# Stick-breaking scores of two heads on the two row halves of TensorE's array, without zero padding

## The reference, cut to what matters

```python
z = jnp.einsum('bqhd,bshd->bhqs', q_blk, k, preferred_element_type=jnp.float32) * scale
valid = key_pos[None, :] < q_pos[:, None]
log_beta = jax.nn.log_sigmoid(z)
log_keep = jnp.where(valid, jax.nn.log_sigmoid(-z), 0.0)
log_keep_after = lax.cumsum(log_keep, axis=3, reverse=True) - log_keep
att = jnp.where(valid, jnp.exp(log_beta + log_keep_after), 0.0)
```

## Time and profile before

| | us |
|---|---|
| median of 3 runs | 1177.25 (1177.04 to 1177.65) |
| the profiled execution, its own time | 1177.26 |
| its span, first to last instruction | 1175.5 |
| TensorE busy | 1156.3 (98%) |
| DVE busy | 812.0 (69%) |
| ACT busy | 627.4 (53%) |
| GpSimd busy | 292.2 (25%) |

### The profile page before, as it was taken

The page is one execution under the profiler, slowest core; times in us unless marked ns, Lnnn a source line. Parts: engine busy times, 40 slices in busy tenths (PEclk is TensorE's granted clock), DMA queues, the critical chain, the costliest instruction groups (busy, mean ns, idle before and its releaser), DMA issues.

```text
span 1175.5 us, 18209 instructions
## 1 busy us (share of the span) xinstructions
PE 1156.3 (98%) x7410; PEld 1033.7 (88%) x7410; DVE 812.0 (69%) x874; ACT 627.4 (53%) x739; POOL 292.2 (25%) x282
## 2 busy tenths in 40 slices
PE   8999999999999999999999999999999999999996
PEld 6998988888998888888899888888889999888885
DVE  7686777675589667776558767766557767767653
ACT  5675565554455556555335656555446755655531
POOL 5000532211123354221111344221110005332221
PEclk9999999999999999999999999999999999999998
DMA  8743445555562345556553345555544335565541
GB/s 314 216 133 108 180 175 188 180 209 187 180 173 105 111 176 214 180 180 215 179 180 141 108 156 206 195 180 201 197 165 175 108 108 180 179 216 179 205 154 36
DMA packets 30828, 201.84 MB, mean 172 GB/s; under 512 B 3504, under 2 KB 4592, under 8 KB 7328
## 3 DMA queue, kind: packets, MB, share of 16 engines
q1 hardware_dynamic: 28800, 197.41, 47.4%
q0 software_dynamic: 352, 1.31, 0.9%
q10 hardware_dynamic: 1600, 2.02, 0.7%
HBM read 197.91 MB, written 1.84 MB: 170 GB/s over the span
## 4 chain that ended last, share of the span: by engine, by line
PE 94%; DVE 4%; ACT 1%; issue 0%; DMA 0%; POOL 0%; DVEq 0%; ACTq 0%
PE banks L1262 41%; PE banks L1266 21%; PE banks L1256 7%; PE banks L1258 7%; PE banks L1257 7%; PE banks L1250 4%; PE banks L1391 1%; PE banks L1333 1%; PE banks L1405 1%; DVE w_lo L831 1%; DVE x_split L837 1%; PE banks L1393 0%; PE banks L1541 0%; DVE small L1102 0%; DVE scratch L1099 0%
## 5 line engine op out<-in xcount | busy, mean ns | idle before, releaser
L812 DVE TENSOR_TENSOR w_lo<-raw,w_hi 128x2048 fp32r<-128x2048 f32 x180 | 440.9, 2452 | 201.6 <-ACT w_hi L476 201.5
L476 ACT ACTIVATE w_hi<-raw 128x2048 fp32r<-128x2048 f32 x183 | 349.4, 1909 | 95.3 <-PE banks L1266 47.2
L1262 PE MATMUL banks<-x_split,w_hi 128*128 128x512 f32 x1408 | 336.7, 391 | 0.0
L1262 PEld LDWEIGHTS banks<-x_split,w_hi 128*128 128x128 f32 x1408 | 258.5, 188 | 49.9
L1266 PEld LDWEIGHTS banks<-x_split,w_lo 128*128 128x128 f32 x1408 | 181.0, 191 | 7.1
L1266 PE MATMUL banks<-x_split,w_lo 128*128 128x256 f32 x1408 | 184.0, 283 | 0.0
L1262 PE MATMUL banks<-hid_split,w_hi 128*128 128x512 f32 x704 | 173.1, 391 | 0.0
L1262 PEld LDWEIGHTS banks<-hid_split,w_hi 128*128 128x128 f32 x704 | 127.4, 188 | 23.3
L1256 PE MATMUL banks<-x_split,w_hi 128*128 128x256 f32 x384 | 110.5, 288 | 0.0
L1257 PE MATMUL banks<-x_split,w_hi 128*128 128x256 f32 x384 | 108.6, 283 | 0.0
L1258 PE MATMUL banks<-x_split,w_lo 128*128 128x256 f32 x384 | 108.6, 283 | 0.0
(11 more groups left out here) (179 smaller groups left out, 1485.6 us busy)
## 6 DMA issues: line engine op xcount, KB each, us to landing
raw<-w SPq DMA_DIRECT2D x183, 1024.0 KB, 4.9
raw<-w SPq DMA_DIRECT2D x8, 256.0 KB, 6.9
x<-x_in SPq DMA_DIRECT2D x2, 512.0 KB, 5.7
raw<-w SPq DMA_DIRECT2D x2, 512.0 KB, 8.9
out<-x SPq DMA_DIRECT2D x4, 256.0 KB, 2.8
k_all<-k_all ACTq DMA_DIRECT2D x1, 960.0 KB, 12.3
rel_scratch<-rel_lut POOLq DMA_DIRECT2D x1, 768.0 KB, 10.6
rel_bias<-rel_scratch POOLq DMA_DIRECT2D x2, 256.0 KB, 9.0
```

The costliest lines, as they stand in the source:

```text
L476: act.activation(w_hi[slot][:, :], raw[slot][:, :], ACT.Copy).then_inc(hi_done, 1)
L812: dve.tensor_tensor(w_lo[slot][:, :], raw[slot][:, :], w_hi[slot][:, :].bitcast(FP32), ALU.subtract).then_inc(lo_done, 1)
L1262: return pe.matmul(pair(b), wt[0], xs, start=first, stop=False, skip_group_check=True)
```

## The change

The zeros go, and with them GpSimd's `query_zeros`. Queries and keys of a pair lie in one buffer `qk_both`, are split by one instruction on ACT and one on DVE into `qk_split`, and each head's score matmuls use only its own 64 rows (`own(h)`): 64 x 128 weights (the keys) on one row half of the array. The products are issued in twos: early keys of one head (256 columns) into the early bank and late keys of the other head into the late bank, on the other row half. The late ones have 128 queries; these are streamed twice, to 256 columns, and the second copy goes to a part of the bank that nobody reads. Three such twos cover early keys of head 0 and late keys of head 1. Then TensorE waits for its own two last matmuls (`z_half`), and three more cover early keys of head 1 and late keys of head 0. ACT's `soft` waits for the two last matmuls of the second group (`z`).

```diff
--- before.py
+++ after.py
@@ -127,8 +127,8 @@
         q_all = placed("q_all", [P, HEADS, SEQ], FP32, 0)
         k_all = placed("k_all", [P, HEADS, SEQ], FP32, 4 * HEADS * SEQ)
         v_all = placed("v_all", [P, 2, D], FP32, 8 * HEADS * SEQ)
-        q_split = placed("q_split", [P, 2, 2, SEQ], FP32R, 4 * KT * SEQ)
-        k_split = placed("k_split", [P, 2, SEQ], FP32R, 4 * HEADS * SEQ + 4 * KT * SEQ)
+        qk_both = placed("qk_both", [P, 2, SEQ], FP32, 0)
+        qk_split = placed("qk_split", [P, 2, 2, SEQ], FP32R, 4 * KT * SEQ)
         hid_split = placed("hid_split", [P, FFN_T, 2, SEQ], FP32R, 0)
         o_split = sb("o_split", [P, KT, 2, SEQ], FP32R)
         o_hi, o_lo = o_split[:, :, 0, :], o_split[:, :, 1, :]
@@ -275,12 +275,12 @@
         norm = signals("norm", "six x_new hi lo ss sums ms guess rstd")
         latent = signals("lat", "c_new hi lo ss sums ms guess rstd")
         mixer = [
-            signals("m0", "v_new qk_new q_zero k_hi q_hi k_lo q_lo z ln softplus sp_lo sums att av o_hi o_lo"),
+            signals("m0", "v_new qk_new qk_hi qk_lo z_half z ln softplus sp_lo sums att av o_hi o_lo"),
             signals("m1", "q_part q_new rope_tab rot_in krope_sum krope_new kfill k_part k_new v_part v_new logits max_new "
                           "exp_new sum_new inv_new p_new pt pt_new av o_hi o_lo"),
             signals("m2", "q_tmp q_new v_new v_part logits s_new s_max m_new exp_new sink_new r_new p_new pt pt_new av "
                           "o_hi o_lo"),
-            signals("m3", "v_new qk_new q_zero k_hi q_hi k_lo q_lo z ln softplus sp_lo sums att av o_hi o_lo"),
+            signals("m3", "v_new qk_new qk_hi qk_lo z_half z ln softplus sp_lo sums att av o_hi o_lo"),
         ]
         ffn = signals("ffn", "g_part g_free g_new u_part u_new silu scaled hid hi lo acc")
 
@@ -405,19 +405,6 @@
                             pool.tensor_scalar(pr[:, a, keys], pr[:, a, keys], s[:, 12 + 2 * late + a:13 + 2 * late + a],
                                                1.0, ALU.mult, ALU.mult).then_inc(m.p_new, 1)
 
-            def query_zeros(i):
-
-                if i:
-                    pool.wait_ge(norm.x_new, 16 * i)
-                pool.wait_ge(norm.ss, 2 * i + 1)
-                if i == 0:
-                    pool.wait_ge(cast_done, 2)
-                for h in range(2):
-                    if h:
-                        pool.wait_ge(mixer[i].q_zero, 1)
-                    pool.memset(q_split[others(h), :, h, :].bitcast(FP32), 0.0).then_inc(mixer[i].q_zero, 1)
-                pool.wait_ge(mixer[i].q_zero, 2)
-
             def swa_products():
                 m = mixer[2]
                 for g in range(GROUPS):
@@ -443,8 +430,6 @@
                 model_squares(2 * i)
                 if i == 0:
                     masks()
-                if i % 3 == 0:
-                    query_zeros(i)
                 if i == 0:
                     relative_bias()
                 if i == 1:
@@ -527,9 +512,7 @@
 
                 def qk_hi(p):
                     act.wait_ge(m.qk_new, 2 * p + 2)
-                    act.activation(k_split[:, 0, :], k_all[:, p, :], ACT.Copy).then_inc(m.k_hi, 1)
-                    for h in range(2):
-                        act.activation(q_split[own(h), 0, h, :], q_all[own(h), p, :], ACT.Copy).then_inc(m.q_hi, 1)
+                    act.activation(qk_split[:, 0, :, :], qk_both[:, :, :], ACT.Copy).then_inc(m.qk_hi, 1)
 
                 qk_hi(0)
                 split(b + 7)
@@ -540,7 +523,7 @@
                 def soft(p):
 
                     e, z = buf(0, 768), two_banks[p % 2][:, 0:768]
-                    act.wait_ge(m.z, p + 1)
+                    act.wait_ge(m.z, 2 * p + 2)
                     t = step(act.activation(e, z, ACT.Abs))
                     act.wait_ge(act_step, t)
                     t = step(act.activation(e, e, ACT.Exp, scale=-1.0))
@@ -907,21 +890,17 @@
 
                     dve.wait_ge(unit_used, b + 5 + p)
                     src = bank[4 + p % 2]
-                    dve.scalar_tensor_tensor(q_all[:, p, :], src[:, 0:SEQ], SB_SCALE, R, ALU.mult,
+                    dve.scalar_tensor_tensor(qk_both[:, 0, :], src[:, 0:SEQ], SB_SCALE, R, ALU.mult,
                                              ALU.mult).then_inc(m.qk_new, 1)
-                    dve.tensor_tensor(k_all[:, p, :], src[:, SEQ:512], R, ALU.mult).then_inc(m.qk_new, 1)
+                    dve.tensor_tensor(qk_both[:, 1, :], src[:, SEQ:512], R, ALU.mult).then_inc(m.qk_new, 1)
 
 
                 sp_hi, sp_lo = soft_split[:, 0, :], soft_split[:, 1, :]
 
                 def qk_low(p):
-                    dve.wait_ge(m.k_hi, p + 1)
-                    dve.tensor_tensor(k_split[:, 1, :], k_all[:, p, :], k_split[:, 0, :].bitcast(FP32),
-                                      ALU.subtract).then_inc(m.k_lo, 1)
-                    for h in range(2):
-                        dve.wait_ge(m.q_hi, 2 * p + h + 1)
-                        dve.tensor_tensor(q_split[own(h), 1, h, :], q_all[own(h), p, :],
-                                          q_split[own(h), 0, h, :].bitcast(FP32), ALU.subtract).then_inc(m.q_lo, 1)
+                    dve.wait_ge(m.qk_hi, p + 1)
+                    dve.tensor_tensor(qk_split[:, 1, :, :], qk_both[:, :, :], qk_split[:, 0, :, :].bitcast(FP32),
+                                      ALU.subtract).then_inc(m.qk_lo, 1)
 
                 qk(0)
                 qk_low(0)
@@ -1372,26 +1351,36 @@
 
                 def logits(p):
 
-                    early, late = score_banks(p)
+                    early, late = bank[2 * (p % 2)], bank[2 * (p % 2) + 1]
                     mask = head_blocks(mask_b[:, 0:512])[:, :, 0, :]
                     pe.matmul(head_blocks(early)[:, :, 0, :], ident_b[:, :], mask, start=True, stop=False,
                               skip_group_check=True)
-                    pe.matmul(late, ident_b[:, :], mask, start=True, stop=False, skip_group_check=True)
-                    if p == 0:
-                        pe.wait_ge(m.q_zero, 2)
-                    for key_low, query_low in ((0, 0), (1, 0), (0, 1)):
-                        if query_low:
-                            pe.wait_ge(m.q_lo, 2 * p + 2)
-                        elif key_low:
-                            pe.wait_ge(m.k_lo, p + 1)
-                        else:
-                            pe.wait_ge(m.q_hi, 2 * p + 2)
-                            pe.wait_ge(m.k_hi, p + 1)
-                        kk, qq = k_split[:, key_low, :], q_split[:, query_low, :, :]
-                        pe.matmul(early, kk[:, 0:P], qq.rearrange("p h s -> p (h s)"), start=False, stop=query_low == 1,
-                                  skip_group_check=True)
-                        last = pe.matmul(late, kk[:, P:SEQ], qq[:, :, P:SEQ], start=False, stop=query_low == 1,
+                    pe.matmul(late[:, 0:SEQ], ident_b[:, :], mask, start=True, stop=False, skip_group_check=True)
+
+                    def early_keys(h, key_low, query_low):
+                        return pe.matmul(early[:, SEQ * h:SEQ * h + SEQ], qk_split[own(h), key_low, 1, 0:P],
+                                         qk_split[own(h), query_low, 0, :], start=False, stop=query_low == 1,
                                          skip_group_check=True)
+
+                    def late_keys(h, key_low, query_low):
+                        twice = qk_split[own(h), query_low, 0, P:SEQ].unsqueeze(1).to_broadcast([HD, 2, P])
+                        spots = late[:, :].rearrange("p (d h q) -> p d h q", d=2, h=2)[:, :, h, :]
+                        return pe.matmul(spots, qk_split[own(h), key_low, 1, P:SEQ], twice, start=False,
+                                         stop=query_low == 1, skip_group_check=True)
+
+                    pe.wait_ge(m.qk_hi, p + 1)
+                    for first in range(2):
+                        if first:
+                            pe.wait_ge(m.z_half, 2 * p + 2)
+                        for key_low, query_low in ((0, 0), (1, 0), (0, 1)):
+                            if key_low and not first:
+                                pe.wait_ge(m.qk_lo, p + 1)
+                            one = early_keys(first, key_low, query_low)
+                            last = late_keys(1 - first, key_low, query_low)
+                        if not first:
+                            one.then_inc(m.z_half, 1)
+                            last.then_inc(m.z_half, 1)
+                    one.then_inc(m.z, 1)
                     last.then_inc(m.z, 1)
 
                 def keep_sums(p):
```

## The result

| | before | after |
|---|---|---|
| median, us | 1177.39 (1177.04 to 1177.73, 8 runs) | 1180.88 (1180.64 to 1181.23, 8 runs) |
| ratio to before | | 1.0030 (95% interval 1.0021 to 1.0039) |
| span of the profiled execution | 1175.5 | 1178.8 |

The change makes the kernel 3.5 us slower; forecast were 3.3. The spans of the two profiled executions differ by 3.3. The page after, busy engines, answers to the earlier trace rows: TensorE has 96 matmuls more (16 steps with 12 score matmuls instead of 6), DVE and ACT 32 instructions less each, GpSimd its four memsets less.

A forecast was written before the change was run, and what follows sets the result against it. TensorE, busy for 98% of the span, was taken as the bound. A step's scores take 1.24 us against 1.06; sixteen steps give +2.9, two returns at p = 0 +0.4, together +3.3: 1180.6 us, range 1175.2 to 1182.4.

The forecast's parts named there:

- the covers: Splits on ACT and DVE, GpSimd's zeros: hidden behind TensorE's `qk` work, so some 0.5 us less a pair is worth nothing.
- The overlap: Score matmuls on two row halves: two fp32r matmuls of 256 columns take the time of one, 0.12 us a pair.
- Rival 1: Score pairs: halves don't overlap in fp32r, a pair takes 0.24 us, 11.5 us more in all, 1192.1 us; chance 0.10.
- low end: Lower case of the sum: pace 0.11 at four places, release 0.03; +0.12 us a step, 1179.6 us in all.
- The change of division: From 128-row masks into half-row scores: load and drain not hidden, 0.20 us each, first pair 0.31 us behind the mask.
- The wait half-way: TensorE waits for its own matmuls between third and fourth pair: 0.45 us instead of 0.12.
- rival 2: Half-way wait nearly free: third to fourth pair 0.12 us, 1175.2 us in all; chance 0.10.
- rival 3: Fourth pair's weight loads pass the half-way wait: 0.11 us a step saved, 1178.8 us in all; chance 0.08.
- Rival 4: Neither the half-way wait nor the entry into the scores costs anything: 1171.6 us; chance 0.06, with anything else faster.
- the entry: New change of array division from the masks into the scores, 16 times, at 0.20 us.
- the release: Half-way wait, from the matmuls' modelled end to the held load: taken as 0.05 us, bounds 0.03 and 0.12.
- The sentence on the Trainium skill's rule (87 ns): Half-way wait: increments of concurrent tiles serialize, 87 ns for two of each instead of 0.05 us; total then 1181.2 us.

The follow-up runs named there:

- run 3: Changed kernel with three splits again on ACT and three on DVE instead of one each: 1180.67 us, ratio 1.0029.
- run 5: Changed kernel with the late queries streamed once (128 columns) instead of twice: 1180.85 us, ratio 1.0029.
- run 2: Changed kernel with both matmuls of a pair on one row half, late scores of the wrong head: 1191.51 us, ratio 1.0120.
- run 1: Changed kernel without half-way wait and bank hand-over; second group reuses the first's rows, half the scores of the wrong head: 1175.08 us, ratio 0.9982.
- run 10: Kernel before plus a TensorE wait for its own first product, the only wait ahead of the second (low-keys wait moved earlier): 1182.46 us, ratio 1.0044.
- run 4: Changed kernel with one increment instead of two at the half-way wait, on the last matmul alone: 1180.28 us, ratio 1.0026.
- run 6: Changed kernel with a bank for each head and no half-way wait, sums in four matmuls a part instead of three: 1177.54 us, ratio 1.0002.
- run 7: Version with a bank per head and no half-way wait, late queries also streamed once: 1176.48 us, ratio 0.9993 against the kernel before.
- run 8: Kernel before plus a TensorE wait, after its first product, for its own last matmul on 128 rows, one increment: 1183.58 us, ratio 1.0052.
- run 11: Changed kernel with one half-way increment, plus a long-met wait on another semaphore written behind the half-way wait: 1180.31 us, ratio 1.0026.

## Why the prediction was right

**The bound and the covers.** TensorE's order set the time, as the earlier trace rows said. The work taken off ACT and DVE is worth nothing (run 3). For GpSimd's zeros no run was made; before, nothing waited for them. Softplus's last piece is ready 1.04 us before the sums want it for p > 0, before 1.07. The second copy of the late queries slows nothing (run 5).

**The overlap** of two fp32r matmuls of 256 columns, which the trace of before showed only for plain fp32, holds: 0.12 us a pair, 0.24 on one half (run 2). Rival 1 is out, and its 11.5 us were 10.6. (The prediction's 0.78 us for 15 loads are 0.10 us per two and not 0.11; only its low end uses this.)

**The change of division** came out at the forecast 0.31 us from the mask to the first pair.

**The wait half-way** was right in kind. It is TensorE's wait for itself that costs, and the cost goes when wait and hand-over go (run 1: 5.8 us). The hand-over of banks is only why the kernel has the wait: without any hand-over and on 128 rows the wait costs 5.3 us, against 5.2 for the halves with the same single increment (run 10; run 4 less run 1). Rivals 2 and 3 are out: third to fourth pair are 0.47 us, not 0.12 or 0.34. Rival 4 goes with them, as both the wait and the entry cost what was forecast or more. What the prediction quotes of the Trainium skill for rival 3 asks for row groups that don't conflict, but the fourth pair uses the same two as the third, so it gave the rival less than the prediction says. The wait's size was forecast a little low. The term is the release, taken as 0.05 between bounds of 0.03 and 0.12; it measured 0.09, of which 0.03 belong to the second increment (run 4). The sentence on the Trainium skill's rule (87 ns) had the better number, and by it the sum was 1181.2.

**The sum.** The release was 0.04 us too small, but other parts of the step were a little too large (third to fourth pair 0.47, forecast 0.45), so the step from second mask to last pair grew by 0.20 us, not 0.18: 16 x 0.02 = 0.3 us more than forecast. On the other side a small stall vanished that the prediction had not seen. In the kernel before, TensorE was held 0.08 us at p = 0 in the sums, on the low part of softplus. DVE's L941 writes it and ends at 50.92, and the load follows at 50.97; from the matmul's start at 50.99 to the next at 51.31 are 0.32 us, where it is 0.24 otherwise. The timeline of the kernel before:

```profile
49.97 0.95 DVE L941 TENSOR_TENSOR soft_split<-scratch,soft_split 128x768 fp32r<-128x768 f32 x1
...
50.97 0.19 PEld L1405 LDWEIGHTS banks<-soft_split,neg_sums 128*128 128x128 f32 x1
50.99 0.48 PE L1405 MATMUL banks<-soft_split,neg_sums 128*128 128x512 f32 x1
...
51.31 0.28 PE L1406 MATMUL banks<-soft_split,neg_sums 128*128 128x256 f32 x1
```

And of the kernel after:

```profile
51.34 0.40 PE L1394 MATMUL banks<-soft_split,neg_sums 128*128 128x512 f32 x1
...
51.58 0.28 PE L1395 MATMUL banks<-soft_split,neg_sums 128*128 128x256 f32 x1
```

There `qk` starts 0.2 us later behind the scores, so softplus is ready in time; twice 0.08 us came back, once in each layer. The forecast's statement that TensorE's matmuls never wait there but before `values` was not quite true: the wait was too short for the table. From mask to mask a step with p > 0 is 0.19 us longer in the traces, and one with p = 0 0.31 us (8.39 against 8.07); for 14 and 2 of them that makes 3.3 us, which is the difference of the spans. Forecast 1180.6, measured 1180.88. The mechanism was right; that the time came out this close is in part luck, as two small errors went opposite ways.

**What would have paid.** The halves themselves save: 2.1 us without the wait (run 1). The layout spends it. Early keys of both heads in one bank and late keys in the other make each half write both banks in turn, and so the wait for the matmuls' end (0.28 us), a release (0.09) and a load that nothing hides (0.11) lie in the middle of every step. A bank for each head avoids that, but gives most of it back in the sums, which then need two matmuls where one wrote both heads: run 6 is level with the kernel before, run 7 0.7 us under it, within its interval.

## What to carry to other kernels

Two matmuls of 64 rows side by side take half the time only while nothing stops TensorE: count the changes of division (0.20 us each here) and above all the waits of TensorE for itself (0.35 us each) against what they save. Give each row half a PSUM bank of its own, so that no hand-over is needed. Where such a wait must be, let one matmul alone signal it, and let it be the only wait ahead of the next load, or the one that is written first.

## What the runs showed of the hardware

- A wait of TensorE for its own matmul costs the same on 64 and on 128 rows: the load follows 0.06 us behind the modelled end with one increment (runs 4 and 10), 0.09 with two that end together (the changed kernel), and the weights are another 0.11 us.
- A wait that holds costs 0.06 us more when it has a semaphore instruction of its own (51 ns) instead of being carried by the load (hold 0.12 in run 8, 0.06 in runs 10 and 11; 1183.58 against 1182.46 us).
- fp32r matmuls of 128 columns keep the pace per column of long ones where no load is in the way: two in a row 0.06 us apart (run 6).
